# Seven block products for two of eight gate and up tile pairs in a feed-forward loop

## The reference, cut to what matters

```python
D_FF = -(-(8 * D_MODEL) // (3 * 256)) * 256      # 5632
...
h2 = rms_norm(x, norm2_w[l]) * (1.0 + sc2) + sh2
ff = (jax.nn.silu(h2 @ w_ffn_gate[l]) * (h2 @ w_ffn_up[l])) @ w_ffn_down[l]
x = x + g2 * ff
```

## Time and profile before

| | |
|---|---|
| median of 3 runs | 2235.67 us (2235.11 to 2240.11) |
| the profiled execution's own time | 2236.0 us |
| its span, first to last instruction | 2234.3 us |
| TensorE busy | 2220.6 us (99%) |
| VectorE busy | 1623.7 us (73%) |
| ScalarE busy | 1103.8 us (49%) |
| GpSimd busy | 136.8 us (6%) |
| granted TensorE clock, mean | 0.998 of full speed |

### The profile page before, as it was taken

The page is one execution under the profiler, slowest core; times in us unless marked ns, Lnnn a source line. Parts: engine busy times, 40 slices in busy tenths (PEclk is TensorE's granted clock), DMA queues, the critical chain, the costliest instruction groups (busy, mean ns, idle before and its releaser), DMA issues.

```text
span 2234.3 us, 31225 instructions
## 1 busy us (share of the span) xinstructions
PE 2220.6 (99%) x10287; PEld 1849.4 (83%) x10287; DVE 1623.7 (73%) x2120; ACT 1103.8 (49%) x1437; POOL 136.8 (6%) x259
## 2 busy tenths in 40 slices
PE   9999999999999999999999999999999999999998
PEld 8888888888888888888888888888888888888886
DVE  6767777878875876888788777766665666666576
ACT  6555446666664445433466554444444443344444
POOL 1100110000000000010011110000000000000000
PEclk9999999999999999999999999999999999999999
DMA  8878896656665765697589987666766776766664
GB/s 321 326 246 308 309 338 234 219 196 210 219 218 193 287 230 195 234 332 268 191 303 324 303 293 253 242 210 213 235 222 231 238 241 228 238 232 223 211 218 147
DMA packets 157899, 551.78 MB, mean 247 GB/s; under 512 B 19441, under 2 KB 25328, under 8 KB 156288
## 3 DMA queue, kind: packets, MB, share of 16 engines
q1 hardware_dynamic: 112416, 405.92, 52.7%
q0 software_dynamic: 34304, 129.64, 16.7%
q10 hardware_dynamic: 11104, 15.22, 2.0%
HBM read 534.92 MB, written 10.53 MB: 244 GB/s over the span
## 4 chain that ended last, share of the span: by engine, by line
PE 96%; DVE 2%; DMA 1%; ACT 1%; issue 0%; SPq 0%; DVEq 0%; ACTq 0%
PE ps L2091 23%; PE ps L2092 23%; PE ps L2093 23%; PE ps L2209 6%; PE ps L2211 6%; PE ps L2210 6%; PE ps L2130 2%; PE ps L2339 1%; DMA raw<-ws_dram 1%; PE ps L2106 1%; PE ps L2108 1%; PE ps L2107 1%; DMA late<-wa_dram 1%; DVE w_lo L1197 0%; PE ps L2269 0%; PE ps L2533 0%
## 5 line engine op out<-in xcount | busy, mean ns | idle before, releaser
L1197 DVE TENSOR_TENSOR w_lo<-raw,w_hi 128x1024 fp32r<-128x1024 f32 x757 | 921.0, 1223 | 513.3 <-ACT w_hi L675 499.2
L675 ACT ACTIVATE w_hi<-raw 128x1024 fp32r<-128x1024 f32 x749 | 788.5, 1060 | 970.9 <-PE ps L2093 820.4
L2091 PE MATMUL ps<-w_hi,a_hi 128*128 128x512 f32 x1612 | 629.3, 390 | 0.1
L2093 PE MATMUL ps<-w_hi,a_lo 128*128 128x512 f32 x1612 | 627.5, 389 | 0.0
L2092 PE MATMUL ps<-w_lo,a_hi 128*128 128x512 f32 x1612 | 627.3, 389 | 0.0
L2093 PEld LDWEIGHTS ps<-w_hi,a_lo 128*128 128x128 f32 x1612 | 302.6, 188 | 63.3
L2091 PEld LDWEIGHTS ps<-w_hi,a_hi 128*128 128x128 f32 x1612 | 302.7, 188 | 62.8 <-DVE w_lo L1197 0.3
L2092 PEld LDWEIGHTS ps<-w_lo,a_hi 128*128 128x128 f32 x1612 | 302.7, 188 | 61.8
L2209 PE MATMUL ps<-w_hi,a_hi 128*128 128x512 f32 x640 | 256.0, 400 | 1.9 <-ACT gst L769 1.9
L2211 PE MATMUL ps<-w_hi,a_lo 128*128 128x512 f32 x640 | 250.3, 391 | 0.0
L2210 PE MATMUL ps<-w_lo,a_hi 128*128 128x512 f32 x640 | 250.0, 391 | 0.0
(11 more groups left out here) (366 smaller groups left out, 2263.3 us busy)
## 6 DMA issues: line engine op xcount, KB each, us to landing
raw<-ws_dram SPq DMA_DIRECT2D x768, 512.0 KB, 4.3
ada<-wa_dram POOLq DMA_DIRECT2D x140, 512.0 KB, 4.8
late<-wa_dram POOLq DMA_DIRECT2D x35, 512.0 KB, 5.4
late_c<-wa_dram POOLq DMA_DIRECT2D x17, 512.0 KB, 5.2
gates_spill<-gst ACTq DMA_DIRECT2D x16, 512.0 KB, 5.6
fT<-fz ACTq DMA_DIRECT2D x160, 32.0 KB, 2.6
ga<-gates_spill POOLq DMA_DIRECT2D x8, 512.0 KB, 4.2
gb<-gates_spill POOLq DMA_DIRECT2D x8, 512.0 KB, 5.6
```

The costliest lines, as they stand in the source:

```text
L675: act.activation(w_hi[:, k.slot(RING), :], raw[:, k.slot(RING), :], ACT.Copy).then_inc(hi_done, 1)
L1197: dve.tensor_tensor(w_lo[:, k.slot(RING), :], raw[:, k.slot(RING), :], w_hi[:, k.slot(RING), :].bitcast(F32), ALU.subtract).then_inc(lo_do ...
L2091: pe.matmul(o, hi(m, tb), w_hi[:, s, cols], start=m == 0, stop=False)
L2093: mm = pe.matmul(o, lo(m, tb), w_hi[:, s, cols], start=False, stop=m == of * kts - 1)
```

## The change

In each of the nine turns the tiles now come in the order gate q, up q for q = 0 to 7. For q = 2 and q = 5 (`QUADS`) the two k-slices, the two token blocks and the two matrices form 2x2 blocks, and the eight block products are replaced by seven: with A the activation blocks and B the weight blocks,

- S1 = A21 + A22, S2 = S1 - A11, S3 = A11 - A21, S4 = A12 - S2 (once, ahead of the loop: `act_mix`, split into `mix_s_hi`, `mix_s_lo`)
- T1 = B12 - B11, T3 = B22 - B12, T2 = B22 - T1, and B21 - T2 (in each turn: `mixed_sums`, four 128x512 subtractions on VectorE into `mix_w`; ScalarE rounds them into `mix_hi`, VectorE subtracts the rest into `mix_lo`, 128x2048 in one instruction)

Three of the products go to PSUM banks of their own (4 to 7 hold four with A11·B11), which the down products use later in the turn. They are added to the gate and up banks through `g_part` and `u_part` in SBUF by VectorE. Gate and up sums keep one bank pair each (`gate_bank`, `up_bank`), the down products alternate between banks 4, 5 and 6, 7; new semaphores (`gate_up_free`, `down_free`, `parts_free`) say what has been drained. Silu reads `g_part` instead of PSUM. The transposes come at the end of the turn's gate and up part (`turn_lanes`), the 16 DMAs are issued from GpSimd's queue (`send_f`), and `act_hi` and `act_lo` stand after steps 3 and 4 of the next turn. VectorE's turn is written out step by step. The last gate and up pass keeps its old tile order; `rows_turn(3)` moves behind its second tile.

```diff
+QUADS = (2, 5)
+MIXED_END = 2 * QUADS[-1] + 2
...
@@ GpSimd's queue
-            with pool.Fori(1, KT) as i:
-                for k in range(2):
-                    pool.wait_ge(ada2_used, 2 * i + (k - 1))
-                    pool.dma_start(ada3[:, k, :], wa[2 * i + (ADA0["ff"] + k)]).then_inc(ada2_landed[k], 16)
+            def send_f(sent):
+                pool.wait_ge(f_lanes, sent)
+                pool.sem_inc(f_asked, 1)
+                for b in range(4):
+                    for i in range(4):
+                        pool.dma_start(turned[32 * b:32 * b + 32, i], lanes[32 * i:32 * i + 32, b]).then_inc(f_turned, 16)
...
+            send_f(1)
+            with pool.Fori(1, turns_ff) as j:
+                for m in range(n):
+                    load_ada2(At(2 - n + m, n, j))
+                send_f(At(1, 1, j).n)
...
@@ ScalarE
-            def steps_sending_f(k, j):
...
+            def mixed_hi(j, n):
+                sums0 = At(4 * len(QUADS) * (j.base - 1) + 4 * n, 4 * len(QUADS) * j.per, j.i)
+                act.wait_ge(w_mix_sum, (sums0 + 2).n)
+                act.activation(mix_hi[:, 0:2], mix_w[:, 0:2], ACT.Copy)
+                act.wait_ge(w_mix_sum, (sums0 + 4).n)
+                act.activation(mix_hi[:, 2:4], mix_w[:, 2:4], ACT.Copy)
...
+                for p in range(4):
+                    step(p)
+                act_hi(j + -1)
+                for p in range(4, 2 * T_K - 1):
+                    step(p)
+                    if p + 1 == MIXED_END:
+                        act.wait_ge(tile_used, (k + MIXED_END).n)
+                        act.activation(g_part[:, 0], ps[:, 4, :], ACT.Copy).then_inc(first_copied, 1)
+                act.wait_ge(act_ready, j.n)
+                act.wait_ge(gate_up_free, At(2 * j.base + 1, 2 * j.per, j.i).n)
+                act.activation(f_silu[:], g_part[:, 0:3:2], ACT.Silu).then_inc(silu_done, 1)
...
@@ VectorE
+            def mixed_sums(k, j, n, freed):
...
+                for x in (k, k + 1):
+                    dve.wait_ge(raw_landed[x.slot(RING)], x.lap(RING, 16))
+                dve.wait_ge(tile_used, freed.n)
+                dve.tensor_tensor(mix_w[:, 0], u[:, 0:NC], g[:, 0:NC], ALU.subtract).then_inc(w_mix_sum, 1)
+                dve.tensor_tensor(mix_w[:, 1], u[:, NC:TW], u[:, 0:NC], ALU.subtract).then_inc(w_mix_sum, 1)
+                dve.wait_ge(w_mix_sum, (sums0 + 1).n)
+                dve.tensor_tensor(mix_w[:, 2], u[:, NC:TW], mix_w[:, 0], ALU.subtract).then_inc(w_mix_sum, 1)
+                dve.wait_ge(w_mix_sum, (sums0 + 3).n)
+                dve.tensor_tensor(mix_w[:, 3], g[:, NC:TW], mix_w[:, 2], ALU.subtract).then_inc(w_mix_sum, 1)
+
+            def mixed_lo(k):
...
+                dve.wait_ge(hi_done, (k + 1).n)
+                dve.tensor_tensor(mix_lo[:], mix_w[:], mix_hi[:].bitcast(F32), ALU.subtract)
+                dve.tensor_tensor(w_lo[:, slot, NC:TW], raw[:, slot, NC:TW], w_hi[:, slot, NC:TW].bitcast(F32), ALU.subtract)\
+                    .then_inc(lo_done, 1)
...
+                step(0)
+                modulated(0)
+                step(1)
+                step(2)
+                step(3)
+                modulated(1)
+                step(4)
                 act_lo(j + -1)
+                step(5)
...
+                step(9)
+                modulated(2)
+                step(10)
+                step(11)
+                modulated(3)
+                dve.wait_ge(first_copied, j.n)
+                part0 = At(2 * j.base - 2, 2 * j.per, j.i)
+                dve.tensor_tensor(g_part[:, 1], ps[:, 6, :], g_part[:, 0], ALU.add).then_inc(part_sum, 1)
+                dve.wait_ge(part_sum, (part0 + 1).n)
+                dve.tensor_tensor(g_part[:, 2], ps[:, 7, :], g_part[:, 1], ALU.add).then_inc(part_sum, 1)
+                step(12)
+                dve.wait_ge(part_sum, (part0 + 2).n)
+                dve.tensor_tensor(u_part[:], ps[:, 5, :].unsqueeze(1).to_broadcast([P, TB, NC]), g_part[:, 1:3], ALU.add)\
+                    .then_inc(parts_free, 1)
+                step(13)
...
+                dve.tensor_tensor(g_part[:, 0:3:2], gate_bank, g_part[:, 0:3:2], ALU.add).then_inc(gate_up_free, 1)
+                step(14)
+                dve.wait_ge(tile_used, (k + 2 * T_K).n)
+                dve.tensor_tensor(u_part[:], up_bank, u_part[:], ALU.add).then_inc(gate_up_free, 1)
...
+                dve.tensor_tensor(f_act[:], u_part[:], f_silu[:], ALU.mult).then_inc(act_ready, 1)
+                step(15)
+                dve.wait_ge(act_ready, (j + 1).n)
+                turn_lanes()
+                dve.wait_ge(down_free, At(4 * j.base, 4 * j.per, j.i).n)
+                for c in range(4):
+                    step(2 * T_K + 2 * c)
+                    b = 4 + 2 * (c % 2)
+                    dve.wait_ge(tile_used, (k + (2 * T_K + (c + 1) * T_Q)).n)
+                    dve.tensor_tensor(acc[:, c], ps[:, b:b + 2, :], acc[:, c], ALU.add).then_inc(down_free, 1)
+                    step(2 * T_K + 2 * c + 1)
...
@@ TensorE
+            def mixed_quad(k, n):
...
+                pe.wait_ge(lo_done, (k + 1).n)
+                product(ps[:, 4, :], ah(2 * q, 0), al(2 * q, 0), w_hi[:, g, 0:NC], w_lo[:, g, 0:NC], first, last)
+                product(gate_bank[:, 0], ah(2 * q + 1, 0), al(2 * q + 1, 0), w_hi[:, g, NC:TW], w_lo[:, g, NC:TW])\
+                    .then_inc(tile_used, 1)
+                pe.wait_ge(lo_done, (k + 2).n)
+                product(up_bank[:, 0], mix_s_hi[:, n, 3], mix_s_lo[:, n, 3], w_hi[:, u, NC:TW], w_lo[:, u, NC:TW])
+                product(gate_bank[:, 1], ah(2 * q + 1, 1), al(2 * q + 1, 1), mix_hi[:, 3], mix_lo[:, 3])
+                mixed(ps[:, 5, :], 0, 0, opens=first, closes=last)
+                mixed(ps[:, 7, :], 2, 1, opens=first, closes=last)
+                mixed(ps[:, 6, :], 1, 2, opens=first, closes=last).then_inc(tile_used, 1)
...
+            for u in range(2):
+                pe.wait_ge(gate_up_free, 2 * (FC - 1) - 1 + u)
+                pe.wait_ge(acc_free, (g + (u + 1)).n)
+                for n in range(T_K):
+                    tile(k + (u * T_K + n), pair(g + u), n, T_K, ah, al)
+                    if u == 0 and n == 1:
+                        pe.wait_ge(down_free, 4 * (FC - 1))
+                        rows_turn(3, 5 * KT, 6 * KT)
```

More of the change, by code:

```diff
@@ L1469, in _ @@
             dve.sem_inc(gate_used, 1)
+            dve.sem_inc(gate_up_free, 1)
+            dve.sem_inc(down_free, 4)
             link(dve.memset(vcg[:].bitcast(F32), 0.0))
@@ L1950, in act_lo, with turn_lanes @@
                 ins.then_inc(f_split, 1)
[L1952 to L1960, removed]
+            def turn_lanes():
+                for tb in range(TB):
+                    last = dve.transpose(fz[:, :, tb], f_act[:, tb].rearrange("p (k b f) -> p b k f", k=4, b=4))
+                last.then_inc(f_lanes, 1)
             def last_lo():
@@ L2605, in turn_last, with product, mixed @@
                         .then_inc(t_done, 1)
-            def down(k, g, c0, c1, hi, lo):
-                for c in range(c0, c1):
-                    gemm(k + c * T_Q, g + c, hi, lo, T_Q)
-            def ff_chunk(k, g, j):
-                gemm(k, g, ah, al, T_K)
-                gemm(k + T_K, g + 1, ah, al, T_K)
-                pe.wait_ge(f_split, j.n)
+            def mixed_quad(k, n):
+                q = QUADS[n]
+                g, u = k.slot(RING), (k + 1).slot(RING)
+                first, last = n == 0, n == len(QUADS) - 1
+                def product(out, hi, lo, whi, wlo, opens=False, closes=False):
+                    pe.matmul(out, hi, whi, start=opens, stop=False)
+                    pe.matmul(out, hi, wlo, start=False, stop=False)
+                    return pe.matmul(out, lo, whi, start=False, stop=closes)
+                def mixed(out, s, w, **group):
+                    return product(out, mix_s_hi[:, n, s], mix_s_lo[:, n, s], mix_hi[:, w], mix_lo[:, w], **group)
+                pe.wait_ge(lo_done, (k + 1).n)
[8 more added lines that the diff above has]
+                mixed(ps[:, 6, :], 1, 2, opens=first, closes=last).then_inc(tile_used, 1)
@@ new lines, in mixed_chunk @@
+            def mixed_chunk(k, j):
+                for q in range(T_K):
+                    if q in QUADS:
+                        if q == QUADS[0]:
+                            pe.wait_ge(down_free, At(4 * j.base, 4 * j.per, j.i).n)
+                        mixed_quad(k + 2 * q, QUADS.index(q))
+                        continue
+                    for u, bank in enumerate((gate_bank, up_bank)):
+                        if q == 0:
+                            pe.wait_ge(gate_up_free, At(2 * j.base - 1 + u, 2 * j.per, j.i).n)
+                        tile(k + (2 * q + u), bank, q, T_K, ah, al)
+                pe.wait_ge(f_split, j.n)
+                pe.wait_ge(parts_free, j.n)
+                for c in range(4):
+                    b = 4 + 2 * (c % 2)
+                    if c >= 2:
```

(4 more changed lines are left out.)

168 lines of the change are left out of this document (117 added, 51 removed).

## The result

The median of six runs of the changed kernel is 2221.22 us (2220.25 to 2223.16); six runs of the kernel before, the three of the table above among them, have a median of 2234.82 (2232.58 to 2240.11). The ratio is 0.9939 with a 95% interval of 0.9928 to 0.9951.

A forecast was written before the change was run, and what follows sets the result against it. TensorE, busy throughout the loop at 0.2267 us a matmul, was taken as the bound. 2236.0 - 12.24 + 1.0 (first turn) = 2224.8 on the profiled execution, so a median of 2224.5 us; range 2222.8 to 2233.

The forecast's parts named there:

- TensorE's part: Loop matmuls: two pairs in nine turns leave out 54 matmuls at 0.2267 us each, -12.24 us.
- VectorE's account: VectorE's work per turn: grows by 14.1 to 55.8 of 63.9 us (87%), so on average it fits.
- the head of a steady turn: First pair's half split on VectorE: ends at 10.7 us, needed at 12.05, so no stall; upper end 0.8 us in all.
- The first turn: GpSimd's 16 sends hold ScalarE 1 to 4 us, making VectorE late at the second pair: TensorE loses +1.0 us (0 to 2).
- The base of the sum: Starting time: 2236.0 us of the profiled execution, median 0.3 below; low end took 0.6 off for the fastest run.
- (a): VectorE becomes the bound: operations 20% dearer, turn 67.0 us, time 2248; chance 0.11 shared with slow sends at high price.
- (c): Small stalls of 0.5 to 0.9 us at the half split in each turn: 2228 to 2231 us; chance 0.10.
- (b): Slow GpSimd sends: 2230.7 us at 1.0 each (0.13, shared with mixes within 0.2%), 2249 at 1.75 (0.11, shared with VectorE bound).
- The ends: Ahead of and behind the loop: `act_mix`'s extra VectorE work and the moved `rows_turn` cost 0.

The follow-up runs named there:

- ve_one: Changed kernel plus one useless 128x1024 sum on VectorE in each turn, between the first modulation part and the rest of the mixed weights: 2222.94 us, ratio 0.9953.
- ve_two: Changed kernel plus two useless 128x1024 sums on VectorE in each turn, at the same place: 2233.37 us, ratio 0.9998.
- the second comparison: Changed kernel run again, unchanged, against further runs of the kernel before: 2221.68 us, ratio 0.9944.
- ve_one_acc: Changed kernel plus one useless VectorE sum per turn, with the `acc` sums put back behind both splits of a column group: 2231.98 us, ratio 0.9990.
- pairs35: Changed kernel with pairs 3 and 5 in seven products instead of 2 and 5: 2229.95 us, ratio 0.9982.

## Why the prediction was right or wrong

**TensorE's part: right, to the hundredth.** 12.24 us were forecast and 12.24 measured, and 6.12 for one pair. The new products keep the pace of 0.2267.

**VectorE's account and the head of a steady turn: right.** 54.4 us against 55.8, the half split 10.84 after the tick against 10.7, needed at 12.04 against 12.05, the long subtraction 2.29 as forecast. The second pair has 1.97 us left in the second turn (ends at 1636.95, needed at 1638.92), where I had about 2; over turns two to nine it is 1.3 to 2.4. `ve_one` and `ve_two` show from the other side that the margin of the first pair is real and about as wide as laid out by hand. What I laid out was a steady turn, though: in the first turn the first pair has 0.47 us left and the second 0.43. And one wait that I had ruled out for the first pair, and not looked at for the second, was there: the second pair's sums wait for their weights in each turn. VectorE's waits in the changed kernel:

```profile
DVE mix_w L2068 <- DMA raw<-ws_dram: 5.9, 9, 1.2
```

The longest is 1.2 us, in the third turn, which has the least left of turns two to nine (1.3 us).

**The first turn: the failed term of the sum, mis-sized.** I took +1.0 us (0 to 2) for ScalarE held 1 to 4 us. GpSimd's and ScalarE's timelines of the changed kernel:

```profile
1550.79 7.84 POOL L676 DMA_DIRECT2D fT<-fz  x16 [2.67 <-DVE fz L2031]
```

```profile
1560.31 1.16 ACT L1150 ACTIVATE f_hi<-fT 128x512 fp32r<-128x512 f32 x2 [1.05 <-DMA fT<-fz]
```

The 16 sends take 7.84 us, and ScalarE stops for 1.05, the low end; TensorE loses 0. In the nine profiles of kernels with these sends the stop is 1.05 to 3.88 us, just the range forecast. But of the four with the change's two pairs and no useless sum (1.05, 2.00, 2.23 and 3.88) only the last cost TensorE anything, 1.1 us. In the others 0.43, 0.71 and 0.72 us were left at the second pair of the first turn. So the path that I had laid out is there, from the sends over ScalarE and VectorE to the second pair, but in these four profiles it cost 0 three times and 1.1 once, and I had put the middle of the range into the sum.

**The base of the sum: the step that failed for the range.** I set the gain against the three runs shown (median 2235.67) and, for the low end, took off 0.6 for the fastest of them. The six runs of the first comparison, those three among them, have a median of 2234.82, and 25 further runs one of 2234.20, from 2232.82 to 2237.28. The profiled execution, 2236.0, was 1.8 us above the latter, and a wait of 1.9 us for `gst` stood in the earlier trace rows: I read it as a wait outside the loop and thus as no concern, not as a sign that the time around the loop varies. A base of 2234.2 less 12.24 is 2221.96, 0.7 above the 2221.22 measured and 0.3 above the 2221.68 of the second comparison. So of the miss of 3.3 us 1.0 is the first turn and 1.5 the base. The last 0.8 I put down to the scatter of medians of five or six runs, whose single times spread over 1.5 to 2.9 us; no run separates it further.

**The rivals.** (a), VectorE as the bound, isn't seen: it needed 65.3 us of VectorE's work in a turn to eat up the gain, and 54.4 were measured. But `ve_two` loses nearly all of it at 56.5 us of work, by one place in the order. (c), small stalls at the half split in each turn, is what `ve_one_acc` and `ve_two` have, and not the change. (b), slow sends, falls with the group of GpSimd's sends in the changed kernel (busy us, mean ns of one | idle before, releaser):

```profile
L676 POOL DMA_DIRECT2D fT<-fz x160 | 78.4, 498 | 177.1 <-DVE fz L2031 173.1 <-issue 3.7
```

They take 0.498 us each to issue, where I had 0.53, and from issue to landing 3.5 in the middle (1.7 to 4.5), against 2.6 on ScalarE's queue. Two of the ten groups of 16 stop on the way, for 0.95 and 2.73 us, with no releaser in the profile. The same two groups do so in all eight kernels that send from GpSimd's queue in the loop, and nothing waits for them; why they stop no run here shows. The Trainium skill (SBUF — State Buffer, section "SBUF: two separate sides") has a VectorE `tensor_copy` between SBUF buffers stretch a DMA of this queue from about 0.62 to 3.1 us. No send of the changed kernel took over 0.52 us to issue, beside subtractions and sums of VectorE in much of the time. Whether a wide copy would do so no run here shows, as VectorE has none in the loop.

**The ends: right.** From the loop's end to the last instruction it is 2234.3 - 2137.37 = 96.9 us before and 2219.3 - 2122.40 = 96.9 after.

**What stays open.** Why the time ahead of the loop moves by several us between executions. It was only seen to move with the same code (first silu from 1527.5 to 1533.8 us over all profiles); its DMAs were not experimented with. The rest of the time, 1627.7 us over all runs of the old loop and 1627.5 over those of the new, leaves no room for an effect of the change on it above about 1 us.

## What to carry to other kernels

Where one engine works without a gap, price a change to its loop by the starts of its instructions and lay out the neighbour's order by hand at the tightest place; what counts there is the margin in microseconds, not the neighbour's busy share. Spend that margin knowingly: here 1.2 us hid everything, an order of work was worth 1.1 of it and only 0.5 us of time on its own, and two sums of 1.14 per turn cost nearly as much as the change had brought. Lay out the first turn by itself; here it had less than half the margin of the others. And take the base of a sum from as many runs as there are, or, where there are three, don't take the low end of the range from their spread: here the fastest of three lay 0.6 us below their median, and 25 further runs reached 2.9 below it.

## What was not expected of the hardware

A wait of TensorE costs more than the profile draws. TensorE's timeline of `ve_two`, at the half split of the second turn:

```profile
1627.35 0.39 PE L2778 MATMUL ps<-w_hi,a_lo 128*128 128x512 f32 x1
1628.69 0.50 PE L2776 MATMUL ps<-w_hi,mix_s_hi 128*128 128x512 f32 x1 [0.96 <-DVE w_lo L2081]
1629.03 0.39 PE L2777 MATMUL ps<-w_lo,mix_s_hi 128*128 128x512 f32 x1
1629.27 0.40 PE L2778 MATMUL ps<-w_hi,mix_s_lo 128*128 128x512 f32 x1
```

The idle time of 0.96 us is counted from the drawn end of the last matmul, 0.39 after its start; at the pace of 0.2267 the next would have started 0.16 earlier than that, so the matmul is 1.12 us late. And it takes 0.34 to the next start, 0.11 more than the pace; why, no run here shows. So this wait costs 0.96 + 0.16 + 0.11, some 1.25 us with the remainder. The ticks say the same: the second turn of `ve_two` is 65.18 us (1615.53 to 1680.71), 1.26 above the changed kernel's 63.92. The sum fits the other kernels, with 0.29 us more for each wait than is drawn: 5.4 us drawn in nine waits of `pairs35` make 5.4 + 9 x 0.29 = 8.0, as measured, 8.4 in eight of `ve_two` make 10.7 of the 11.2 measured, and 7.0 in eight of `ve_one_acc` make 9.3 of the 9.8 measured. Most of what is missing in these two is the ninth turn, whose lateness isn't drawn. TensorE's timeline of `ve_two` there:

```profile
2083.69 0.39 PE L2778 MATMUL ps<-w_hi,a_lo 128*128 128x512 f32 x1
2084.12 0.50 PE L2776 MATMUL ps<-w_hi,mix_s_hi 128*128 128x512 f32 x1
2084.46 0.39 PE L2777 MATMUL ps<-w_lo,mix_s_hi 128*128 128x512 f32 x1
```

The matmul behind the half split starts 0.43 us after the one before it, 0.20 late, and no wait is shown. In `ve_one` the turns two to eight have no late start, only the slower next one; its timeline in the second turn:

```profile
1623.71 0.49 PE L2776 MATMUL ps<-w_hi,mix_s_hi 128*128 128x512 f32 x1
1624.04 0.39 PE L2777 MATMUL ps<-w_lo,mix_s_hi 128*128 128x512 f32 x1
```

These turns are 64.04 us in the mean where the changed kernel's are 63.92. That is why my expectations for the three kernels with a wait in each turn were too mild: the lateness that I had worked out for a steady turn (0.7 us in `pairs35`, 1.07 in `ve_two`, 1.0 in `ve_one_acc`) is near what the starts show (0.69, 1.12 and 1.08), but the 0.11 behind each wait and the late ninth turn of `ve_two` and `ve_one_acc` were not in it.
